# Forming the state-space way-in matrix directly in its final layout, with B turned and the powers repeated through DRAM

## The reference

```python
def s5_direction(u, a_re, a_im, log_dt, b_re, b_im, c_re, c_im, reverse):
    dt = jnp.exp(log_dt)[:, None]
    mag, ang = jnp.exp(a_re * dt), a_im * dt
    ab_re, ab_im = mag * jnp.cos(ang), mag * jnp.sin(ang)
    ...
    bb_re = coef_re[..., None] * b_re - coef_im[..., None] * b_im
    bb_im = coef_re[..., None] * b_im + coef_im[..., None] * b_re
    bu_re = jnp.einsum('lbgh,gph->lbgp', u, bb_re)
    bu_im = jnp.einsum('lbgh,gph->lbgp', u, bb_im)
    ...
    _, _, xr, xi = lax.associative_scan(combine, (sa_re, sa_im, bu_re, bu_im), reverse=reverse, axis=0)
    return einsum('lbgp,ghp->lbgh', xr, c_re) - einsum('lbgp,ghp->lbgh', xi, c_im)
```

## Time and profile before

| what | value |
| --- | --- |
| time, median of 3 runs | 1327.13 us (1324.11 to 1329.89) |
| the profiled execution, its own time | 1328.03 us |
| its span, first to last instruction | 1326.1 us |
| mean granted TensorE clock | 0.990 |
| DMA over the span | 456.83 MB, 344 GB/s |

### The profile page before, as it was taken

How to read it: one execution, slowest core, us unless ns; L and a number is a source line. 1 busy time by engine, 2 the same in 40 slices (tenths; PEclk the granted TensorE clock), 3 DMA queues, 4 the chain that set the end, 5 groups by cost and what they waited for, 6 DMA issues and landing times.

```text
span 1326.1 us, 15280 instructions
## 1 busy us (share of the span) xinstructions
PE 1261.2 (95%) x6167; PEld 570.1 (43%) x6167; DVE 366.1 (28%) x785; ACT 208.2 (16%) x323; POOL 112.9 (9%) x109
## 2 busy tenths in 40 slices
PE   8999899999889999999999999999999999999996
PEld 3478785868643333333333333333333323333332
DVE  6478582021123111221112111122111111221112
ACT  2031422100311111111111111111111111111111
POOL 4599200010010000000000000000000000000000
PEclk9999899999999999999999999999999999999999
DMA  8533653449845999999999999999999999999995
GB/s 244 169 127 128 141 98 128 159 133 381 322 180 242 410 427 428 427 428 428 427 427 428 429 429 428 428 427 429 429 429 428 427 428 429 428 428 428 428 427 212
DMA packets 55128, 456.83 MB, mean 344 GB/s; under 512 B 4760, under 2 KB 6880, under 8 KB 30512
## 3 DMA queue, kind: packets, MB, share of 16 engines
q1 hardware_dynamic: 51744, 449.74, 82.3%
q0 software_dynamic: 2192, 5.99, 2.8%
q10 hardware_dynamic: 1152, 0.52, 0.2%
HBM read 454.11 MB, written 1.61 MB: 344 GB/s over the span
## 4 chain that ended last, share of the span: by engine, by line
PE 62%; DMA 29%; DVE 5%; ACT 3%; issue 1%; SPq 0%; ACTq 0%; DVEq 0%
PE pt L875 17%; DMA ring<-in_w_e 16%; PE pt L915 12%; DMA stage<-in_w_e 6%; DMA low<-in_w_e 6%; PE pt L476 6%; PE pt L489 6%; PE pt L524 4%; PE pt L456 3%; PE pt L842 3%; PE pt L829 3%; PE pt L537 2%; PE pt L881 1%; ACT wi_ L953 1%; DMA stage<-in_w_in 1%
## 5 line engine op out<-in xcount | busy, mean ns | idle before, releaser
L875 PE MATMUL pt<-ring,hres 128*64 128x512 f32 x1216 | 273.1, 595 | 15.3 <-DMA ring<-in_w_e 15.0
L875 PEld LDWEIGHTS pt<-ring,hres 128*64 128x64 f32 x1216 | 84.0, 137 | 198.7 <-issue 167.0
L915 PE MATMUL pt<-ring,wi_ 128*64 128x512 f32 x640 | 141.7, 595 | 5.4 <-ACT wi_ L953 5.4
L1560 DVE TENSOR_SCALAR hnt<-pt 128x512 f32<-128x512 f32 x32 | 22.1, 692 | 308.1 <-PE pt L875 308.1
L1506 DVE COPY ct_<-ct_ 128x2 f32 (+1 forms) x33 | 5.6, 170 | 363.7 <-PE pt L875 359.2
L875 PE MATMUL pt<-stage,hres 128*64 128x512 f32 x416 | 93.9, 595 | 6.6 <-DMA stage<-in_w_e 6.6
L875 PE MATMUL pt<-low,hres 128*64 128x512 f32 x416 | 93.8, 595 | 5.0 <-DMA low<-in_w_e 5.0
L1122 ACT ACTIVATE hnt<-hnt 128x512 f32<-128x512 f32 x32 | 20.2, 630 | 477.9 <-DVE hnt L1560 477.9
L915 PEld LDWEIGHTS pt<-ring,wi_ 128*64 128x64 f32 x640 | 44.5, 137 | 89.7 <-issue 82.4
L842 PE MATMUL pt<-big,lamb 64*128 64x512 f32 x256 | 63.6, 615 | 0.7 <-ACT big L953 0.7
L829 PE MATMUL pt<-a,ct_ 128*64 128x512 f32 x264 | 62.3, 593 | 0.0
(11 more groups left out here) (312 smaller groups left out, 1272.2 us busy)
## 6 DMA issues: line engine op xcount, KB each, us to landing
ring<-in_w_e SPq DMA_DIRECT2D x116, 2048.0 KB, 40.2
low<-in_w_e SPq DMA_DIRECT2D x38, 2048.0 KB, 41.0
stage<-in_w_e SPq DMA_DIRECT2D x38, 2048.0 KB, 40.1
stage<-in_w_in SPq DMA_DIRECT2D x16, 1024.0 KB, 6.7
stage<-in_w_xkv SPq DMA_DIRECT2D x8, 1024.0 KB, 5.9
stage<-in_w_mix_out SPq DMA_DIRECT2D x4, 1024.0 KB, 4.9
stage<-in_w_xq SPq DMA_DIRECT2D x4, 1024.0 KB, 4.9
stage<-in_w_xo SPq DMA_DIRECT2D x4, 1024.0 KB, 16.2
```

Source lines behind the costliest of these rows:

```text
L875: last = pe.matmul(pt[PC][SLOTS * g:SLOTS * (g + 1), 512 * b:512 * (b + 1)], xT[:, k % 4, k // 4], ring_slot[n][:, c:c + 512], start=(k == ...
L915: last = pe.matmul(pt[PD][SLOTS * h:SLOTS * (h + 1), 512:1024], hT[:, c, g], ring_slot[n][:, D * c + 512 * h:D * c + 512 * (h + 1)], start ...
L1560: dve.tensor_scalar(hg, pt[PC][:, 0:512], GATE_MAX, None, ALU.min).then_inc(m_g2, 1)
```

## The change

- **Powers.** DVE orders the powers of each token of the chunk as `lam_src` (32 partitions; semaphore `lamt`). SP writes them to `lam_dram` (256 KB) and reads them back so that every one of the 16 channels of a token holds them: eight DMAs, each writing 32 KB into each of 16 partitions, 4.19 MB in all, into the place of `lin`.
- **B.** PE turns `bbar` in 8 blocks (`turn_b`, within the slab `v`), ACT copies it to `b_turned`. SP writes it to `b_dram` (512 KB) and reads it back in four quarters (`load_b`), each of eight DMAs of 16 partitions with two rows of 4 KB, 1.05 MB a quarter, into two alternating buffers (`b_rows`).
- **Products.** `way_in` on DVE multiplies them in place, 6 instructions of 1024 columns per quarter, 24 in all, in portions between the parts of the heads' softmax; the first 6 stand ahead of the first `row_max`. `way_in_step`, the eight rounds of turns and their copies are gone; POOL has no share in the way-in.
- **Order.** `lag0_products` stand within the slab `v`. The turns of q and k and `scores(0)` stand ahead of `ga0`, each head's pieces one slab earlier than before. On DVE, `bbar` is formed ahead of the rotation of k.
- **Memory.** The memory tokens `mn` lie in a piece of `ring` that the first `b_rows` and others have used, and their load waits for `lin` 3. The Toeplitz loads wait for `tokp` 4.

The diff, cut to what the prediction speaks of:

```diff
@@ SP @@
+            def load_b(quarter):
+                for t in range(TC):
+                    src = b_dram[2 * quarter:2 * quarter + 2].rearrange("a h n -> h a n")
+                    dst = ring[HG * t:HG * (t + 1), 16384 + 2048 * (quarter % 2):16384 + 2048 * (quarter % 2 + 1)]
+                    sp.dma_start(dst.rearrange("h (a n) -> h a n", a=2), src).then_inc(s_b[quarter % 2], 16)
             for i, (slab, w, r, c) in enumerate(SLOT_USES):
+                if i == SLAB_END["q"] + STAGE:
+                    sp.wait_ge(S["lamt"], 1)
+                    for j in range(4):
+                        sp.dma_start(lam_dram[:, :, j].rearrange("t a n -> a t n"),
+                                     lam_src[8 * j:8 * j + 8].rearrange("g t c m -> g t (c m)")).then_inc(s_lamw, 16)
+                    sp.wait_ge(s_lamw, 4 * 16)
+                    sp.wait_ge(S["taba"], 1)
+                    for t in range(TC):
+                        sp.dma_start(lin_flat[HG * t:HG * (t + 1)],
+                                     lam_dram[t:t + 1].rearrange("t a j n -> t (a j n)").broadcast_to([HG, 8 * 8 * P])).then_inc(s_lam, 16)
+                if i == SLAB_END["k"] + STAGE:
+                    sp.wait_ge(S["bte"], 1)
+                    sp.dma_start(b_dram.rearrange("a h n -> (a h) n"), b_turned).then_inc(s_bw, 16)
+                    sp.wait_ge(s_bw, 16)
+                    load_b(0)
+                    sp.wait_ge(S["rope"], 2)
+                    load_b(1)
+                if i == SLAB_END["v"] + STAGE:
+                    sp.wait_ge(S["lin"], 1)
+                    load_b(2)
+                if i == SLAB_END["ga1"] + STAGE:
+                    sp.wait_ge(S["lin"], 2)
+                    load_b(3)
...
@@ PE @@
-            natural("v", PB, hnT, ("vev", 1))
+            natural("v", PB, hnT, ("vev", 1), inside={(0, 4): turn_b, (1, 0): lag0_products})
...
-            flipped("ga0", PA, hnT, ("gates", 1))
...
             scores(0)
-            flipped("ga1", PB, hnT, ("gates", 2))
+            flipped("ga0", PB, hnT, ("gates", 1))
             turn_probs(0)
             scores(1)
-            flipped("gs0", PB, hnT, ("gates", 3))
+            flipped("ga1", PB, hnT, ("gates", 2))
             values(0)
             turn_probs(1)
             scores(2)
-            flipped("gs1", PB, hnT, ("gates", 4))
+            flipped("gs0", PB, hnT, ("gates", 3))
             values(1)
             turn_probs(2)
             scores(3)
+            flipped("gs1", PB, hnT, ("gates", 4))
+            values(2)
+            turn_probs(3)
+            turn_some(mn, 0, PD, 1)
...
-            pe.wait_ge(S["bp"], 2)
-            for r in range(8):
-                u, read = ((PB, "lta"), (PD, "ltv"))[r % 2]
-                take(u, (read, r // 2 + 1))
-                for i in range(8):
-                    last = turn(pt[u][:, P * i:P * (i + 1)], s5b[:, 4 * r + i // 2, i % 2])
-                last.then_inc(S["ltp"], 1)
-                if r == 1:
-                    turn_probs(3)
...
@@ DVE @@
+            def way_in():
+                for q in range(4):
+                    rows = b_rows[q % 2]
+                    lr, li = (lin[:, 2 * q:2 * q + 2, :, c].rearrange("p a j m -> p (a j) m") for c in range(2))
+                    br, bi = rows[:, :, 0], rows[:, :, 1]
+                    dve.wait_ge(s_b[q % 2], 8 * 16 * (q // 2 + 1))
+                    if q == 0:
+                        dve.wait_ge(s_lam, 8 * 16)
+                        dve.wait_ge(S["bspl"], 1)
+                    dve.tensor_tensor(way_a, lr, br, ALU.mult)
...
-            dve.wait_ge(S["tabp"], 1)
-            way_in(range(0, 1))
-            for h, times in enumerate((range(1, 2), range(2, 3), range(3, WAY_IN_SPLIT), ())):
+            lag0()
+            some_way_in(6)
+            for h, (between, behind) in enumerate(((1, 0), (1, 3), (1, 7), (1, 4))):
                 row_max(h)
+                some_way_in(between)
                 weigh(h)
-                if h == 0:
-                    lag0()
-                way_in(times)
+                some_way_in(behind)
```

More of the change, by code:

```diff
@@ L401, in _ @@
             last.then_inc(S["s5wd"], 1)
[L403 to L412 removed]
+            pool.wait_ge(S["lin"], 3)
             pool.dma_start(mn, T["mem"].rearrange("a (t p) n -> p (a t) n", p=P)).then_inc(s_mem, 16)
@@ L465, in weights, with natural @@
                 return got
-            def natural(slab, u, xT, *who):
+            def natural(slab, u, xT, *who, inside=None):
                 ws = weights(slab)
@@ L472, in natural @@
                     for k in range(4 * len(ws)):
+                        if inside and (t, k) in inside:
+                            inside[(t, k)]()
                         w, loaded, n_loaded = ws[k // 4]
@@ L618, in values @@
                 last.then_inc(S["pvp"], 1)
-            pe.wait_ge(S["bspl"], 1)
-            take(PA, ("kse", 1))
-            for j in range(4):
-                for c in range(2):
-                    last = pe.matmul(pt[PA][:, P * j:P * (j + 1)], bbar[:, c, 8 * j:8 * j + 8], ct[:, c, j],
-                                     start=(c == 0), stop=(c == 1))
-            last.then_inc(S["k0p"], 1)
             pe.wait_ge(S["qka"], 2)
@@ L998, in _ @@
             last.then_inc(S["bspl"], 1)
-            slab_done(act, "ga0")
-            act.wait_ge(S["tabp"], 1)
-            copy(a1[:, 0:1024], unit(PA)).then_inc(S["gates"], 1)
+            slab_done(act, "v")
+            copy(vn, unit(PB, "p (t n) -> p t n", t=NT)).then_inc(S["vev"], 1)
+            act.wait_ge(S["utp"], 1)
+            copy(uT_[:, :], unit(PD)).then_inc(S["uta"], 1)
             act.wait_ge(S["qkp"], 1)
-            copy(t2[:, 1024:2048], unit(PD)).then_inc(S["qka"], 1)
+            copy(t2[:, 1024:2048], unit(PA)).then_inc(S["qka"], 1)
             act.wait_ge(S["qkp"], 2)
@@ L1026, in copy_probs @@
                 copy(wT[:, h % 2], pt[PC][:, 0:512].rearrange("p (k l) -> p k l", k=NT)).then_inc(S["wta"], 1)
-            exps(0)
-            slab_done(act, "ga1")
-            copy(a1[:, 1024:2048], unit(PB)).then_inc(S["gates"], 1)
-            copy_probs(0)
-            exps(1)
-            slab_done(act, "gs0")
-            copy(a2[:, 0:1024], unit(PB)).then_inc(S["gates"], 1)
-            copy_probs(1)
-            exps(2)
-            slab_done(act, "gs1")
-            copy(a2[:, 1024:2048], unit(PB)).then_inc(S["gates"], 1)
-            copy_probs(2)
-            exps(3)
+            gate_slabs = (("ga0", a1[:, 0:1024]), ("ga1", a1[:, 1024:2048]), ("gs0", a2[:, 0:1024]), ("gs1", a2[:, 1024:2048]))
+            for h, (slab, gates) in enumerate(gate_slabs):
+                exps(h)
+                if h == HEADS - 1:
+                    act.wait_ge(s_mem, 16)
+                    for t in range(NT):
+                        act.wait_ge(S["sumsq"], NT + t)
+                        square(mn[:, t], mem_square, 4 + t)
+                    root(4, 6, NT, D, 2 * NT)
+                slab_done(act, slab)
+                copy(gates, unit(PB)).then_inc(S["gates"], 1)
+                copy_probs(h)
             act.wait_ge(S["kp"], 1)
             copy(t1[:, 1024:2048], unit(PB)).then_inc(S["kta"], 1)
-            copy_probs(3)
-            for r in range(0, 8, 2):
-                act.wait_ge(S["ltp"], r + 1)
-                copy(ring[:, 8192 + 1024 * r:8192 + 1024 * (r + 1)], unit(PB)).then_inc(S["lta"], 1)
-                if r < 2 * NT:
-                    t = r // 2
-                    act.wait_ge(s_mem, 16)
-                    square(mn[:, t], ring[:, 20480 + t * D:20480 + (t + 1) * D], 4 + t)
-            root(4, 6, NT, D, 2 * NT)
             act.wait_ge(S["zp"], 1)
@@ L1054, in _ @@
             act.wait_ge(S["kse"], 1)
-            copy(ring[:, 22528:23552], unit(PB)).then_inc(S["zka"], 1)
-            for i, u in enumerate((PB, PD)):
+            copy(ring[:, 22528:23552], unit(PD)).then_inc(S["zka"], 1)
+            for i, u in enumerate((PD, PB)):
                 act.wait_ge(S["ztp"], i + 1)
@@ L1282, in _, with rope @@
             rt2 = ring[:, 18944:19456].rearrange("p (c f i) -> p c f i", c=8, f=2)
-            for n, slab, u, dst in ((1, "q", PB, qn), (2, "k", PA, kn)):
+            def rope(n, slab, u, dst):
                 slab_done(dve, slab)
```

147 lines of the change are left out of this document (77 added, 70 removed).

## The result

| | before | after |
|---|---|---|
| median of the runs | 1328.10 us (4 runs, 1324.11 to 1329.89) | 1347.71 us (4 runs, 1345.88 to 1348.06) |
| ratio | | 1.0147, 95% interval 1.0127 to 1.0166 |
| profiled execution | 1328.0 us, span 1326.1 | 1347.37 us, span 1345.6 |

A forecast was written before the change was run, and what follows sets the result against it. A chain 62% PE and 29% DMA bounds it; shifts ahead of mk0 reach the end. Load waits outweigh the shorter tail: mk0 21.3 us later, 1328.0 to 1349.3, less 0.9 for the profiled run: 1348 us, 8-in-10 range 1322 to 1358.

The forecast's parts named there:

- The rate of the powers' loads: Eight DMAs to 16 partitions each, from about 56 us: 100 GB/s, 4.19 MB in 42 us, to 98 us.
- ordering of the powers: DVE's copies and fills after the rotation of q, ahead of the powers' write: 2.7 us, to 51.3 us.
- ga0: Gate slab on PE, its pieces queued behind the powers: wait of some 20 us, half clock after, end at 118 us.
- B's quarters: SP's loads of turned B, 1.05 MB each at 100 GB/s: first landed at 117.7 us, second at 128.
- Products and softmax: DVE's six first products to 125.3 us, then 5.3 and 0.4 us to `turn_probs(0)` at 131.
- From there: PE after `turn_probs(0)`: no waits through ga1, gs0 and gs1, which ends at 182.6 us.
- a tail: PE from gs1's end to mk0: 13.6 us, where 35.5 us lay before; mk0 at 196.2 us.
- arrives at the end as one: A microsecond lost or won ahead of slab mk0 reaches the end in full: 21.3 us later.
- nothing that absorbs a shift: From mk0 on PE runs on its slabs almost without idle time, so no later part takes up the shift.
- the forecast's own range: Total time if the main forecast holds: 1339 us at 109 GB/s without clock loss, to 1358 at 85 GB/s.
- full rate: Rival: new loads at 428 GB/s, powers landed at 66.6 us, 10.7 us won, 1316 us; chance 0.20.
- Two groups at once: Rival: loads of neighbouring 16-partition groups overlap at 200 GB/s, mk0 at 175.1 us, no change, 1327 us; chance 0.13.
- The slabs overtake: Rival: ga0's pieces served beside the powers, only DVE waits, `turn_probs(0)` at about 117, 1336 us; chance 0.05.

The follow-up runs named there:

- experiment 2: Changed kernel with each of the powers' eight loads writing 16 partitions that lie 8 apart instead of 16 neighbours; 1336.66 us against 1327.11.
- experiment 3: Changed kernel with the powers' eight loads reading 16 different rows of an expert's weights instead of one row 16 times; 1348.67 us against 1327.11.
- experiment 6: Against experiment 5: the one load of 128 partitions reads 128 rows of an expert's weights instead of 16 rows repeated eight times; 1333.9 us against 1325.81.
- experiment 5: Changed kernel with the powers written to DRAM twice and read by one load of 128 partitions, 16 rows repeated eight times; 1338.91 us, 1.0085 of before.
- experiment 1: Changed kernel with the powers' write and eight loads queued behind ga0's two pieces on SP; 1349.64 us, 1.0171 of before.
- experiment 7: On top of experiment 5: B's quarters also read by loads of 128 partitions, 16 rows repeated eight times, two loads a quarter; 1341.42 us against 1328.38.
- experiment 9: Changed kernel with powers written twice, loaded in quarters of 128 partitions between slab pieces, each softmax first, half the memory's turns later; 1319.46 us, 0.9940 of before.
- experiment 4: Changed kernel with the powers' eight loads issued from ScalarE's queue instead of SP's; 1346.68 us against 1326.95.
- experiment 10: Against experiment 9: ScalarE takes the root of the memory's squares behind the last gates and probability copies; 1314.77 us, 0.9906 of before.

## Why the prediction was right, point by point

- **The rate of the powers' loads**, the choice on which the sign hung: 100 GB/s taken, 112 measured. The reason given, that what the new loads share with the Toeplitz loads is the destination and not the run, is what experiments 2 and 3 show. The last of them landed at 96.3 us; forecast were 98 for its data and 1 us more for the signal, a term that no run shows by itself. The rate gave 4.6 us. A later start took back 1.8: DVE was done with the rotation of q 1.4 us earlier than forecast, by the luck of the first two slabs, but its ordering of the powers took 5.1 us where 2.7 were taken, and the write to DRAM 4.4 where 3.7 were.
- **ga0**: forecast to start once its pieces land at 101.5 and to end at 118; it started at 98.90 and ended at 115.5. The wait of about 20 us was 18.35. The half clock behind it came as foreseen: 16.64 us in place of 13.98.
- **B's quarters** were mis-sized: 100 GB/s taken, 127 to 130 measured. The first quarter was there at 112.9, not 117.7. Of these 4.8 us the rate gave 2.2; the other 2.6 had come with B's write, done at 102.7 and not 105.3, behind the faster powers. Products and softmax took 0.7 us less than forecast, and `turn_probs(0)` came at 125.46, not 131, after a wait of 9.93 us, not 13.
- **From there**: after head 0 no wait, as forecast; gs1 ended at 178.2, forecast 182.6; a tail of 13.3 us, forecast 13.6; mk0 at 191.45, forecast 196.2. DVE's last product ended at 174.7, forecast 179, and PE took it up 10.5 us later, not 5; by the forecast's own sum it was 10 as well.
- **The end**: with mk0 at +16.55 us the step "arrives at the end as one" would give 1344.6 for the profiled execution; 1347.37 was measured. The sentence that I had found nothing that absorbs a shift holds, but the shift grew by 2.9 us in the router and first expert, where the granted clock fell at other places. So the sum was 4.75 us too high up to mk0 and 2.9 too low behind it, and that 1348 was met within 0.3 us is luck: the forecast's own range ended at 109 GB/s, with 1339, and the measured 112 lies outside it. The mechanism did not need that luck.
- **The rivals**: "full rate" has its answer in experiment 6. With the powers at 392 GB/s the time was 1334, not 1316: the rival assumed the full rate for B's quarters too, and those stay at 127 to 150 GB/s, going to 16 partitions each. Its products beside POOL, at 1.97 us each, took 2.0 to 2.3. "Two groups at once" was forecast for loads that overlap; the 200 GB/s that it took is what experiments 2 and 5 reach by other means, and there the time is 1337 to 1339 and not 1327: it, too, let B's quarters come at 200 GB/s. "The slabs overtake" did not happen within a queue, and experiment 1, which puts ga0's pieces ahead, shows that it would have been worth nothing: its 1336 rested on `turn_probs(0)` at 117, but quarter 0 also needs B, whose write is queued behind the powers.

## What to carry to other kernels

Before replacing computation by loads, work out a load's rate from the partitions that it writes, not from its bytes: 16 neighbouring partitions moved 112 GB/s where 128 moved 392, if each had a row of its own, and 210 if 8 shared one. The weights behind them waited for the difference, and another queue did not help. When an added transfer makes two waits, follow both back to their source before repairing one; here the larger wait was free and the smaller one, with DVE's order behind it, was the price. And a change that loses time as a whole may hold a gain: the tail's 22 us were real, and with the loads, their order and DVE's and ScalarE's order put right the median came out 13.6 us below before's (1314.77 against 1328.38), or 0.69 to 1.19% by the interval.

## What the runs showed that I had not expected

- A load of all 128 partitions can be slow: 23.6 us for 4.19 MB from 16 rows of DRAM repeated eight times each, 12.1 us from 128 rows of their own (experiments 5 and 6). Why is open. Another form, whose outermost dimension is 8 long, left half of the engines' time unused (experiment 7).
- Loads of 16 neighbouring partitions do not all move alike: 94 to 102 GB/s for the Toeplitz loads, 112 for the powers with runs of 32 KB, 127 to 130 for B's quarters with two runs of 4 KB for each partition. I have no experiment on it.
- Issuing one DMA can hold SP's sequencer: B's write took 12.08 us to issue in after, behind the powers' eight loads and ga0's two pieces, 9.45 in experiment 5, 5.25 in experiment 6, and 1.03 in experiment 9, where one load of 1 MB stood ahead of the pieces. It is not the powers alone: in experiment 1 the write stands directly behind the same eight loads, with the pieces long landed, and takes 0.42; in experiment 4, with the powers in ScalarE's queue, 0.34. So a DMA costs its queue some 0.46 us where little waits ahead of it in that queue; how much is too much no run says.
- The granted clock is not a fixed cost, in the first two slabs (27.7 or 29.4 us, experiment 10) as in the router and the first expert. The shift against before grew behind mk0 by 2.9 us in after, shrank in size by 4.0 in experiment 9 (from -12.0 at mk0 to -8.0 at the end), and stayed in experiment 10. Differences of 3 to 4 us between the profiles of two versions of this kernel can come from it alone.
